# In the sum of layer 0's expert rows, a tile's norm goes ahead of the next tile's halves, and two groups of loads change place

## The reference, cut to what matters

```python
routed = jax.ops.segment_sum(y_rows.reshape(n_rows, d), src, ...)[:n_tok]   # sum of 6 gated rows per token
y = routed + swiglu(h, shared_gu, shared_down)
xc = xc + mod_c[5] * y[:, :n_ctx];  xl = xl + mod_l[5] * y[:, n_ctx:]
...                                                                        # next layer
hl = modulate(rms_norm(xl, norm1_g[l]), mod_l[0], mod_l[1])                 # h * (1 + scale) + shift
hc = modulate(rms_norm(xc, norm1_g[l]), mod_c[0], mod_c[1])
... split_columns(hc @ w_in[l]), split_columns(hl @ w_in[l]) ...
```

## Time and profile before

| | us |
|---|---|
| three runs | 2820.43, 2813.58, 2818.83 |
| their median | 2818.83 |
| the profiled execution | 2823.65 |
| its span, first to last instruction | 2821.5 |
| TensorE busy in it | 2429.6 (86%) |
| VectorE, ScalarE, GpSimd busy | 740.9, 444.1, 323.1 |

### The profile page before, as it was taken

The page is one execution under the profiler, slowest core; times in us unless marked ns, Lnnn a source line. Parts: engine busy times, 40 slices in busy tenths (PEclk is TensorE's granted clock), DMA queues, the critical chain, the costliest instruction groups (busy, mean ns, idle before and its releaser), DMA issues. The chain is left out here.

```text
span 2821.5 us, 36781 instructions
## 1 busy us (share of the span) xinstructions
PE 2429.6 (86%) x15205; PEld 1332.8 (47%) x15205; DVE 740.9 (26%) x1589; ACT 444.1 (16%) x901; POOL 323.1 (11%) x380
## 2 busy tenths in 40 slices
PE   4998999999998998989884898998897889888885
PEld 2457854555444444444431366865443334343332
DVE  1363444353111111111102445453311111111111
ACT  1232243210000000000000132342000000000000
POOL 0005300000111111110100004400011111010000
PEclk8999999999999999999997899999999999999998
DMA  8000077434999999999985310013799999999993
GB/s 300 30 15 32 3 302 305 178 142 148 396 425 420 407 401 403 387 408 391 410 339 212 116 45 17 3 64 139 274 404 427 420 422 421 416 409 415 411 412 133
DMA packets 126587, 775.99 MB, mean 275 GB/s; under 512 B 36760, under 2 KB 45096, under 8 KB 69968
## 3 DMA queue, kind: packets, MB, share of 16 engines
q1 hardware_dynamic: 103376, 735.75, 64.6%
q0 software_dynamic: 23040, 37.82, 3.6%
HBM read 770.98 MB, written 44.44 MB: 289 GB/s over the span
## 5 line engine op out<-in xcount | busy, mean ns | idle before, releaser
L1418 PE MATMUL banks<-arena,htreg 128*64 128x384 f32 (+1 forms) x4288 | 933.3, 526 | 177.0 <-DMA arena<-in_exp_w_gu 170.1
L1418 PEld LDWEIGHTS banks<-arena,htreg 128*64 128x64 f32 (+1 forms) x4288 | 458.6, 158 | 621.7 <-issue 402.5
L1439 PE MATMUL banks<-arena,modreg 128*64 128x512 f32 (+1 forms) x1608 | 433.8, 600 | 23.8 <-issue 19.7
L2159 DVE TENSOR_TENSOR modreg<-modreg,banks 128x384 f32<-128x384 f32 x80 | 44.3, 554 | 1063.5 <-ACT modreg L1721 1059.9
L1439 PEld LDWEIGHTS banks<-arena,modreg 128*64 128x64 f32 (+1 forms) x1608 | 153.9, 148 | 246.9 <-issue 242.7
L2468 POOL DMA_INDIRECT htreg<-h_d,lsg x74 | 76.2, 1030 | 1068.2 <-PE banks L1399 925.5
L988 PE MATMUL banks<-arena,htreg 128*128 128x512 f32 (+3 forms) x480 | 159.7, 492 | 0.0
L2314 DVE COPY modreg<-banks 128x512 f32<-128x512 f32 x74 | 51.2, 692 | 321.0 <-PE banks L1439 321.0
L1721 ACT ACTIVATE modreg<-banks 128x384 f32<-128x384 f32 x80 | 39.3, 492 | 579.8 <-PE banks L1418 579.8
L2474 POOL DMA_INDIRECT y_d<-modreg,lst x74 | 73.4, 992 | 479.3 <-DVE modreg L2314 478.7
L988 PEld LDWEIGHTS banks<-arena,htreg 128*128 128x128 f32 x480 | 90.0, 191 | 65.5 <-issue 61.5
(11 more groups left out here) (393 smaller groups left out, 2276.7 us busy)
## 6 DMA issues: line engine op xcount, KB each, us to landing
arena<-in_exp_w_gu SPq DMA_DIRECT2D x256, 1536.0 KB, 23.1
arena<-in_exp_w_down SPq DMA_DIRECT2D x128, 1536.0 KB, 23.3
arena<-in_w_mod SPq DMA_DIRECT2D x32, 1024.0 KB, 9.8
arena<-y_d SPq DMA_DIRECT2D x6, 3072.0 KB, 16.7
modreg<-in_w_mod SPq DMA_DIRECT2D x14, 1024.0 KB, 7.6
modreg<-mod_d SPq DMA_DIRECT2D x20, 512.0 KB, 6.0
arena<-in_w_in SPq DMA_DIRECT2D x4, 2048.0 KB, 9.4
arena<-in_w_out SPq DMA_DIRECT2D x2, 4096.0 KB, 14.1
```

Of the source, the lines that this page charges most:

```text
L1418: last = mm(gu_bank(n, half)[rows, 0:DE], src[:, k, rows], up4[q][:, i, DE * half:DE * (half + 1)], start=(k == 0), stop=(k == KD - 1))
L1439: last = mm(ps[4 + half][rows, :], actT[:, k, rows], dn3[q][:, k, 512 * half:512 * half + 512], start=(k == 0), stop=(k == KE - 1))
```

## The change

In SP's order the four shift and scale pieces are issued behind the second block instead of the third, and the small rows and taps ahead of the waits and of the projection weights instead of behind them. In VectorE's order the norm of tile i - 1 is finished between the sixth rows of tile i and its halves, instead of behind the halves; the wait for the shift and scale pieces moves into the first `finished`.

```diff
@@ SP @@
-                    if i == YB - 1 and l + 1 < DEPTH:
+                    if i == 1 and l + 1 < DEPTH:
                         load_mod(l + 1, 0, range(2))
                 if l + 1 < DEPTH:
+                    load_small(l + 1)
                     sp.wait_ge(y_added.sem, y_added.at(l, YB))
                     sp.wait_ge(out_psum.sem, out_psum.at(2 * l + 1, 2 * YB))
                     load_projection(l + 1)
-                    load_small(l + 1)
                     phase_end(sp, "sp")
@@ VectorE, finished(i) @@
                     u, s = 2 * (l + 1), i // 2
+                    if i == 0:
+                        dve.wait_ge(mod_loaded.sem, mod_loaded.at(u, 4))
                     dve.wait_ge(std_ready.sem, std_ready.at(u, i + 1))
@@ VectorE, the loop over tiles @@
                     stt(acc[:, t, :], yrow[i % YB][:, BY_PE, :], gate[:, i, BY_PE:TOPK], acc[:, t, :], ALU.mult, ALU.add
                         ).then_inc(y_added.sem, 1)
+                    if i and l + 1 < DEPTH:
+                        finished(i - 1)
                     dve.wait_ge(y_added.sem, y_added.at(l, i + 1))
...
                     if l + 1 < DEPTH:
-                        if i == 0:
-                            dve.wait_ge(mod_loaded.sem, mod_loaded.at(2 * (l + 1), 4))
-                        else:
-                            finished(i - 1)
                         dve.wait_ge(squares_ready.sem, squares_ready.at(2 * (l + 1), i + 1))
```

## The result

| | us |
|---|---|
| predicted | 2799.8 (2793 to 2808) |
| measured, median of 6 runs | 2799.03 (2788.86 to 2804.86) |
| the kernel before, median of its runs beside it | 2815.81 |
| ratio, with its 95% interval | 0.9934 [0.9915, 0.9953] |
| the profiled execution and its span | 2795.47, 2793.3 |

The kernel became faster by 0.66%. Two later comparisons of the same pair gave 0.9954 [0.9937, 0.9970] and 0.9932 [0.9915, 0.9949]: 13 to 19 us.

A forecast was written before the change was run, and what follows sets the result against it. A relay between TensorE and VectorE was taken to bound the phase. Terms 9.3 + 4.6 + 5.5 - 0.4 gave 19.0 us; 2823.65 less 19.0, less 4.8 for the median, is 2799.8 (2793 to 2808).

The forecast's parts named there:

- The relay: Between the layers, TensorE sums a tile, VectorE finishes the previous norm, TensorE transposes it, then sums the next; 20.2 us waits.
- the rival in which transfers share: Third block's packets mix with the shift and scale pieces, which land as late as now; gain 15.9, 2802.9 us, chance 0.12.
- A turn: VectorE's full cycle for one tile, residual to residual, forecast at 9.50 us.
- my 0.04 behind L1830: VectorE's gap after L1830, counted in each turn: 1.32 us with its gap where the row has 1.28.
- The collision: Tile 1's L1837 on VectorE meets GpSimd's fourth diagonal and ends 1.0 us later; bounds 0 and 1.25.
- VectorE sets the pace: VectorE turns to tile 3's second half at about 1554.7, after TensorE has summed tile 3 at 1552.9.
- the worst end: On SP, the taps wait for the fourth block to land at 1541.3 and end at 1548.3.
- Rival two and three: SP's issue ends last: two, slow L764, 2815.1 us, chance 0.06; three, taps stretched too, 2827.3 us, chance 0.02.
- their slow case: On SP, L764 takes 27.64 us instead of 10.03, and the taps are stretched by the same 2.8 times.
- the clock's: On TensorE, 5.5 us gained from the clock: 4.2 on tiles 2 and 3, 1.3 on transposes.
- The wait terms: On TensorE, gains of 9.3 us for tile 0's wait and 4.6 for the wait ahead of tile 1's transposes.

The follow-up runs named there:

- order_only: The kernel after with both groups of loads back in place, so only VectorE's order is changed; ratio 0.9967, phase 71.7 us.
- loads_only: The kernel after with VectorE's order as before, so only both groups of loads are moved; ratio 0.9981, phase 74.2 us.
- small_only: The kernel before with only the small rows and taps moved ahead of the waits and projection weights; ratio 1.0000, phase 77.6 us.
- rows_third: The kernel after with the shift and scale pieces put back behind the third block; ratio 0.9945, phase 63.8 us.
- small_ahead: The kernel after with the small rows and taps issued ahead of the fourth block instead of behind it; ratio 0.9947, phase 64.0 us.
- diag_late: The kernel after, with GpSimd's fourth diagonal waiting for tile 1's residual; ratio 0.9931, phase 60.1 us.

## Why the prediction was right, point by point

*What bounds the phase.* The relay was the right reading. `order_only` alone shortens it by 6.8 us (78.5 to 71.7), `loads_only` by 4.4, `small_only` by nothing that can be told, and all together by 17.1. The parts alone sum to about 11, since each opens what the others held: without the small loads' move 4.4 us are lost to SP, without the pieces' move 2.4. Taken one after the other they sum up: 78.5, with VectorE's order 71.7 (`order_only`), with the small loads' move as well 63.8 (`rows_third`), with the pieces' move as well 61.4.

*The load order.* I put the pieces at 24.0 us into the phase and the third block at 31.05. The last piece was issued by 1497.95 and landed after 20.1 at the latest, at most 24.8 us in; the third block was issued at 1497.99 and landed after 27.0, at 1525.0, 31.7 us in. It is in time for tile 2 (1525.49) by half a microsecond, and the pieces landed ahead of it as issued: the rival in which transfers share falls. That half microsecond is the exception. In the seven other profiles with this order of the blocks and VectorE's new order, tile 2 starts within some 0.1 us of the third block's landing; in `small_ahead`, where it lands latest (28.1 us after issue), TensorE stands idle 1.63 us ahead of it. It costs nothing there, as VectorE comes to tile 2's sums without a wait, but on TensorE the block has no slack. The views are those of the tensor mod_d and of the transfers issued near 1498:

```profile
DMA to landing us min/median/max: 17.9/18.3/20.1
```

```profile
arena<-y_d SPq DMA_DIRECT2D x1, 3072.0 KB, 27.0
```

*VectorE's order.* From the first issue, forecast against measured: the norm of tile 0 starts at 27.0 against 28.4; tile 1's residual is ready at 34.9 against 36.1 (1529.44); the last norm ends at 58.3 against 59.1 (1552.44). The start was late by 1.3, because the first block landed 11.4 us after issue instead of 10.96 and the first tiles took 20.10 instead of 19.25. A turn was 9.3, not 9.50 (my 0.04 behind L1830 isn't there: the reciprocal starts before it has ended), which gave 0.4 back in two turns. The collision was 1.62 - 0.69 = 0.93 against my 1.0, and `diag_late` shows it on the path in full. By the Trainium skill (SBUF — State Buffer, "SBUF: two separate sides") a VectorE operation with two SBUF inputs and a GpSimd operation that reads SBUF exclude each other. The trace agrees again: L1841 starts 0.19 behind the diagonal and ends 0.55 behind its end, and with the diagonal elsewhere it takes 0.69.

*TensorE.* Tile 2 was to start 31.35 us in and did at 32.2. From the first transpose to the next matmul it is 0.87 and 0.93 us where I had 1.1. A tile at full clock takes 8.75 where I had 8.6. VectorE sets the pace, by 0.47 us where I had 0.3.

*SP.* Rows and taps were stalled, not to the worst end: they ended 42.4 us in, between my 34.4 and 45.4, and 1.4 behind tile 2's sums. SP was done 55.8 us in and ScalarE 61.8. Rival two and three fall; neither L764 (10.32) nor the taps (6.14) came near their slow case.

*The sum.* The forecast put the phase at 61.0, and it is 61.9, 61.2 and 61.1, in the mean 0.4 more. The gain was forecast as 19.0 and is 17.1 by the profiles, so 1.5 of the 1.9 missing lie in the kernel before: its phase is 80.0 in the one profile I had, 78.5 in the mean of three. The term that was too large is the clock's: 4.2 us for the cold starts of tiles 2 and 3, from one profile in which they took 10.78 and 10.60. In two others of that order tile 2 takes 9.32 and 9.41, tile 3 9.87 and 9.91. With 8.75 for a tile at full clock the term is 3.9 in the profile on record, 1.7 and 1.8 in the others, 2.5 in the mean. The wait terms (9.35 and 4.89) came back within 0.01 in each of these profiles.

That the time came within 0.8 us of the forecast is luck. I subtracted from a median of 2818.83, and with three more runs beside it that median is 2815.81, 3.0 lower; the gain by the medians is 16.8, 2.2 less than mine. The two errors cancel, and six runs of the kernel after spread over 16 us.

## What to carry to other kernels

When two engines hand tiles back and forth, look at what stands between a hand-over and its use in the order of the slower one: moving three operations ahead of six, with none saved, took 6.8 of 78.5 us off this phase by itself. Cost the queue in the same step, for a phase that shrinks soon ends with a load issue that had been covered by 2 us. And take a cold-clock term from several executions, since waits repeat and the clock's share doesn't.

## What the runs showed of the hardware that I had not expected

- The time at the low clock after an idle stretch varies between executions: behind the same 9.35 us of idle and the same transposes, the 20 instructions of tile 2 took 10.78 and 9.32 us in two executions of the kernel before and 9.41 in `small_only`.
- SP's issue of the same tiny loads took differently long by their place: ten rows and six tap columns took 12.3 us behind the projection weights, 13.4 behind three blocks of which one was still landing, and 19.0 with a fourth 3 MB block queued; the stalls fall on single issues (in the kernel after 3.48, 3.62 and 1.56 us instead of 0.43). Why they are shortest behind the weights no run here shows.
